# Raw memory rows into the first projections, their row norm behind them, and the first transfers reordered

## What is computed

```
def rms_norm_2(x, gain):
    y = xf * lax.rsqrt(jnp.mean(xf * xf, axis=-1, keepdims=True) + EPS)
    return y * gain
mem_kv = rms_norm_2(mem, mem_norm) @ mem_wkv            # 256 x 1024 @ 1024 x 2048
mem_k, mem_v = jnp.split(mem_kv, 2, axis=-1)
mem_k = rms_norm_2(mem_k.reshape(bsz, MEM_LEN, MEM_HEADS, MEM_HEAD_DIM), mem_knorm)
```

## Time and profile before

| what | value |
|---|---|
| median of 3 timed runs | 1941.95 us (1940.13 to 1942.1) |
| profiled execution, its own time | 1947.68 us |
| its span, first to last instruction | 1945.9 us |
| mean granted TensorE clock | 0.975 |
| TensorE busy | 1867.0 us, 96% of the span |
| VectorE busy | 1265.8 us, 65% |
| ScalarE busy | 898.9 us, 46% |
| GpSimd busy | 109.9 us, 6% |
| moved by the transfers | 311.34 MB, 160 GB/s in the mean |

### The profile page before, as it was taken

The page is one execution under the profiler, slowest core; times in us unless marked ns, Lnnn a source line. Parts: engine busy times, 40 slices in busy tenths (PEclk is TensorE's granted clock), DMA queues, the critical chain, the costliest instruction groups (busy, mean ns, idle before and its releaser), DMA issues.

```text
span 1945.9 us, 31345 instructions
## 1 busy us (share of the span) xinstructions
PE 1867.0 (96%) x12538; PEld 1681.6 (86%) x12551; DVE 1265.8 (65%) x1569; ACT 898.9 (46%) x1082; POOL 109.9 (6%) x79
## 2 busy tenths in 40 slices
PE   6988999998999998999999999999999998899999
PEld 6975899987589997999898888999999987789998
DVE  5786877788787677555667655555655567556555
ACT  5544544444454445333554455333433357545332
POOL 0300200030020000000034000000000000000000
PEclk9996999999699999999999999999999998999999
DMA  9540465554046554555442544555555542335553
GB/s 299 187 140 13 145 223 178 175 162 147 8 146 217 193 176 134 191 193 177 132 148 87 202 166 138 188 193 180 177 194 176 190 152 87 110 107 174 183 183 129
DMA packets 227044, 311.34 MB, mean 160 GB/s; under 512 B 6614, under 2 KB 199414, under 8 KB 226326
## 3 DMA queue, kind: packets, MB, share of 16 engines
q1 hardware_dynamic: 224038, 298.07, 45.9%
q0 software_dynamic: 2640, 10.66, 1.7%
q10 hardware_dynamic: 288, 1.54, 0.2%
HBM read 307.09 MB, written 3.15 MB: 159 GB/s over the span
## 4 chain that ended last, share of the span: by engine, by line
PE 88%; DVE 6%; ACT 4%; issue 2%; DMA 1%; DVEq 0%; ACTq 0%
PE bank L681 46%; PE bank L937 18%; PE bank L833 7%; PE bank L704 4%; PE bank L690 3%; PE bank L1003 1%; PE bank L979 1%; PE bank L737 1%; DVE w_lo L2038 1%; DVE work L2035 1%; ACT w_hi L1473 1%; DVE work L2038 1%; PE bank L990 1%; DVE x L2035 1%; PE bank L1127 1%
## 5 line engine op out<-in xcount | busy, mean ns | idle before, releaser
L2038 DVE TENSOR_TENSOR w_lo<-raw,w_hi 128x2048 fp32r<-128x2048 f32 x280 | 643.5, 2307 | 343.7 <-ACT w_hi L1473 343.2
L1473 ACT ACTIVATE w_hi<-raw 128x2048 fp32r<-128x2048 f32 x280 | 532.8, 1904 | 675.7 <-PE bank L681 431.9
L681 PE MATMUL bank<-xt_hi,w_hi 128*128 128x256 f32 x2544 | 723.4, 284 | 4.9 <-DVE w_lo L2038 3.3
L681 PE MATMUL bank<-xt_hi,w_lo 128*128 128x256 f32 x2544 | 721.2, 283 | 0.0
L681 PE MATMUL bank<-xt_lo,w_hi 128*128 128x256 f32 x2544 | 721.1, 283 | 0.0
L681 PEld LDWEIGHTS bank<-xt_hi,w_hi 128*128 128x128 f32 x2544 | 489.0, 192 | 9.3 <-issue 3.7
L681 PEld LDWEIGHTS bank<-xt_lo,w_hi 128*128 128x128 f32 x2544 | 489.0, 192 | 2.4 <-issue 0.2
L681 PEld LDWEIGHTS bank<-xt_hi,w_lo 128*128 128x128 f32 x2544 | 488.9, 192 | 0.0
L937 PE MATMUL bank<-w_hi,act_hi 128*128 128x512 f32 x528 | 206.5, 391 | 0.0
L937 PE MATMUL bank<-w_lo,act_hi 128*128 128x512 f32 x528 | 206.2, 390 | 0.0
L937 PE MATMUL bank<-w_hi,act_lo 128*128 128x512 f32 x528 | 205.5, 389 | 0.0
(11 more groups left out here) (307 smaller groups left out, 2108.6 us busy)
## 6 DMA issues: line engine op xcount, KB each, us to landing
raw<-in_ffn_wi SPq DMA_DIRECT2D x88, 1024.0 KB, 5.1
raw<-in_ffn_w_up SPq DMA_DIRECT2D x44, 1024.0 KB, 5.1
raw<-in_ffn_wo SPq DMA_DIRECT2D x44, 1024.0 KB, 4.9
raw<-in_ffn_w_down SPq DMA_DIRECT2D x22, 1024.0 KB, 5.4
raw<-in_w_in SPq DMA_DIRECT2D x14, 1024.0 KB, 5.4
raw<-in_ssd_in_proj SPq DMA_DIRECT2D x14, 1024.0 KB, 5.2
raw<-in_mem_wkv SPq DMA_DIRECT2D x9, 1024.0 KB, 8.1
raw<-in_w_out SPq DMA_DIRECT2D x8, 1024.0 KB, 5.1
```

What stands on the lines that cost most here:

```text
L681: ins = first(mm(dst, w[s][:, k, c0:c0 + m], xt[v][:, k, :], start=k == 0 and p == 0, stop=k == KT - 1 and p == 2))
L1473: return act.activation(dst, src, ACT.Copy)
L2038: return dve.tensor_tensor(out=out, in0=in0, in1=in1, op=op)
```

## The change

The memory rows are turned as they land, without their norm. The gain of each feature is applied as before, when the banks are emptied. The norm of a row is the same factor r for all of a row's products, so it can be applied later. For the values, tokens lie on partitions, and ScalarE multiplies by r (`rcol`) while it empties the bank, in two instructions instead of one. For the keys, r drops out of the norm of each head if epsilon is divided by r squared: TensorE adds epsilon times (mean square of the row + epsilon), held in `vcol`, to each mean of squares by two products of the broadcast column with the identity, and the root is taken without a bias. The sums of squares and their root move on ScalarE behind the splits of mem0 and mem1; VectorE's reciprocal moves behind its own.

SP issues mem0 right behind `memx`, ahead of the small parameters, and then waits until mem0 has landed before it issues mem1. ScalarE issues the constants behind the split of mem0. The early parameters are turned into bank 4 instead of bank 0.

```diff
--- before.py
+++ after.py
@@ -523,6 +523,7 @@
         row_ready = sem("row_ready")
         qsum_ready = sem("qsum_ready")
         even_rows = sem("even_rows")
+        mem_scale = sem("mem_scale")
         gain_ready = sem("gain_ready")
         zgate_ready = sem("zgate_ready")
 
@@ -861,8 +862,12 @@
                     ins.then_inc(bank_full[b], 1)
 
                 pe.wait_ge(early_in, 16 * EARLY_DMAS)
-                turn_parameters(0, 0, range(1))
-                turn(memx, "mem")
+                turn_parameters(4, 0, range(1))
+                for b in range(4):
+                    claim(b, f"mem.t{b}")
+                pe.wait_ge(memx_in, 16)
+                for tt, h in ORDER:
+                    turn_half(memx, tt, h)
                 turned("mem")
                 for j in range(4):
                     pair_fm(f"mem{j}", j % 2, f"memk{j}")
@@ -883,8 +888,13 @@
                 pe.wait_ge(sq_ready, seen.next(sq_ready))
                 b = 4 + h % 2
                 claim(b, f"{tag}.ms{h}")
+                pe.wait_ge(mem_scale, 1)
+                for tt in range(TT):
+                    mm(bank[b][:, P * tt:P * tt + P], vcol[:, tt:tt + 1].broadcast_to([P, P]), ident,
+                       start=True, stop=False, skip_group_check=True)
                 for c in range(2):
-                    ins = mm(bank[b][:, 0:T], cst("mean256"), sq[:, 2 * h + c, :], start=c == 0, stop=c == 1)
+                    ins = mm(bank[b][:, 0:T], cst("mean256"), sq[:, 2 * h + c, :], start=False, stop=c == 1,
+                             skip_group_check=True)
                 ins.then_inc(bank_full[b], 1)
 
             def norm(tag, l):
@@ -1521,13 +1531,6 @@
             def start():
                 act.dma_start(con[:, 0:P], consts[:, 0:P]).then_inc(ident_in, 16)
                 act.wait_ge(ready, 1)
-                act.wait_ge(memx_in, 16)
-                act.dma_start(con[:, P:], consts[:, P:cols["pick"][0]]).then_inc(const_in, 16)
-                for tt in range(TT):
-                    step(act.activation(z[:, tt, :], memx[:, tt, :], ACT.Square, accum_out=st[:, tt:tt + 1]))
-                    act.activation(st[:, 2 + tt:3 + tt], st[:, tt:tt + 1], ACT.Sqrt, scale=1.0 / D,
-                                   bias=eps[:, 1:2]).then_inc(sd_ready, 1)
-
                 def take_parameters(first, n):
                     b = full(f"par{first}")
                     drained(f"par{first}", copy(par[:, first:first + n, :], b[:, 0:P * n]))
@@ -1535,8 +1538,13 @@
 
                 take_parameters(0, 1)
                 split()
+                act.dma_start(con[:, P:], consts[:, P:cols["pick"][0]]).then_inc(const_in, 16)
                 take_stream("mem", lambda k: par_col("mem_norm_2", k))
                 split()
+                for tt in range(TT):
+                    step(act.activation(z[:, tt, :], memx[:, tt, :], ACT.Square, accum_out=st[:, tt:tt + 1]))
+                act.activation(st[:, 2:2 + TT], st[:, 0:TT], ACT.Sqrt, scale=1.0 / D,
+                               bias=eps[:, 1:2]).then_inc(sd_ready, 1)
                 for j in range(9):
                     if j < 8:
                         split()
@@ -1545,7 +1553,11 @@
                         drained(f"memk{j - 1}", copy(mem_k[:, 2 * j - 2:2 * j, :], b[:, :]))
                     elif j > 4:
                         b = full(f"memv{j - 5}")
-                        drained(f"memv{j - 5}", copy(mem_v[:, :, 256 * (j - 5):256 * (j - 5) + 256], b[:, :]))
+                        act.wait_ge(mem_scale, 1)
+                        for tt in range(TT):
+                            ins = act.activation(mem_v[:, tt, 256 * (j - 5):256 * (j - 5) + 256],
+                                                 b[:, 256 * tt:256 * tt + 256], ACT.Copy, scale=rcol[:, tt:tt + 1])
+                        drained(f"memv{j - 5}", ins)
                     if j == 3:
                         for tt in range(TT):
                             act.wait_ge(var_ready, seen.next(var_ready))
@@ -1567,7 +1579,7 @@
 
             def deviation(tag, h):
                 b = full(f"{tag}.ms{h}")
-                drained(f"{tag}.ms{h}", act.activation(x_sd[:, h, :], b[:, 0:T], ACT.Sqrt, bias=eps[:, 1:2]))
+                drained(f"{tag}.ms{h}", act.activation(x_sd[:, h, :], b[:, 0:T], ACT.Sqrt))
 
             def norm(tag, l):
                 if tag in ("mix", "ffn"):
@@ -2155,15 +2167,14 @@
                 dve.memset(eps[:, 2:3], 64 * RMS_EPS)
                 dve.memset(a_pad[:, :, :], 0.0)
                 dve.memset(zero[:, :], 0.0).then_inc(ready, 1)
-                for tt in range(TT):
-                    dve.wait_ge(sd_ready, seen.next(sd_ready))
-                    step(dve.reciprocal(rs[:, tt:tt + 1], st[:, 2 + tt:3 + tt]))
-                    dve.tensor_scalar(memx[:, tt, :], memx[:, tt, :], rs[:, tt:tt + 1], None,
-                                      ALU.mult).then_inc(z_ready, 1)
                 taken("par0")
                 split()
                 take_stream("mem", lambda k: par_col("mem_norm_2", k))
                 split()
+                dve.wait_ge(sd_ready, seen.next(sd_ready))
+                dve.reciprocal(rcol[:, :], st[:, 2:2 + TT])
+                dve.tensor_scalar(vcol[:, :], st[:, 0:TT], RMS_EPS / D, RMS_EPS * RMS_EPS, ALU.mult,
+                                  ALU.add).then_inc(mem_scale, 1)
                 for j in range(8):
                     split()
                     if j == 2:
@@ -2848,7 +2859,6 @@
             def start():
                 pool.wait_ge(x_in, 16 * TT)
                 load_wide(inp["ln_in_g"], inp["ln_in_b"])
-                seen.next(z_ready, TT)
 
                 pool.wait_ge(mem_ready, 4)
                 pool.dma_start(mem_dram[0], work[:, WORK - 4096:WORK - 2048]).then_inc(mem_out, 16)
@@ -2986,12 +2996,15 @@
 
             def start():
                 sp.dma_start(memx[:, :, :], inp["mem_2"][0].rearrange("(t p) d -> p t d", p=P)).then_inc(memx_in, 16)
+                columns("mem0", inp["mem_wkv_2"], 0, 256)
                 sp.wait_ge(stage_clear, 1)
                 for dst, src in stage_loads(True):
                     sp.dma_start(dst, src).then_inc(early_in, 16)
+                sp.wait_ge(landed[0], 16)
                 late, sent = stage_loads(False), 0
                 for j in range(8):
-                    columns(f"mem{j}", inp["mem_wkv_2"], 256 * j, 256)
+                    if j >= 1:
+                        columns(f"mem{j}", inp["mem_wkv_2"], 256 * j, 256)
                     if j == 2:
                         for tt in range(TT):
                             sp.dma_start(x[:, tt, :], inp["x"][0, P * tt:P * tt + P, :]).then_inc(x_in, 16)
```

## The result

The changed kernel's median is 1944.25 us (22 runs, 1939.89 to 1950.17) against 1941.09 for the kernel before, measured beside it (22 runs, 1936.13 to 1946.07). The ratio is 1.0023, with a 95% interval of 1.0014 to 1.0032: slower. The medians are 3.2 us apart and the means, of which the ratio is made, 4.5; 2.7 was forecast. Its profiled execution took 1943.42 us with a span of 1941.6, and that span is 4.3 us shorter than the one before.

What follows compares the result with a forecast made beforehand. TensorE, with 88% of the chain, was taken as the bound, so only its stops and added instructions count. +1.0 us at memk3 and +1.7 for products gave +2.7 on 1941.95: 1944.7 us, range 1941.0 to 1946.8.

Steps and rivals of the forecast that it cites:

- the products (+1.7): At the four mean squares, two added products each, 0.43 us a pair, lengthen TensorE's path by 1.7 us.
- the stop at memk3 (+1.0): Ahead of memk3 TensorE waits 1.5 us for memk1's copy, so memk3 begins 1.0 us later than before.
- More than 0.2% slower: Case that the whole kernel gets slower by over 0.2%, which is 3.9 us; chance 0.15.
- Part 1: Start of TensorE: parameters land with mem0, taken as 10.4 us; TensorE starts 0.5 us earlier, at 18.3.
- Part 2: ScalarE's squares, table load and root behind mem1's split, 3.9 us together, are hidden with 1.6 us to spare.
- Part 3: SP's wait for mem0 idles the transfers 3.5 us; mem4 lands 2.45 later, at 36.1, and memk3 begins 1.0 later.
- The hole in the transfers: While SP waits for mem0 before issuing mem1, the engines have nothing from 8.4 to 11.9 us, 3.5 us.
- mem4 is not late: Rival at memk3: wide rows let mem4 go first or the hole is shorter; +1.2 us, 1943.2; chance 0.2.
- Part 4: Products added at the four mean squares put 4 x 0.43 = 1.7 us on TensorE's path; bounds 1.7 and 2.4.

Runs made afterwards that it cites:

- e6: Changed kernel with the first transfers in the order of the kernel before (parameters, mem0, mem1 without wait), norm still deferred: median 1941.64 us, ratio 1.0007.
- e8: e6 with one pair of epsilon products, added by VectorE, and memk0 to memk3 emptied ahead of the next split: median 1942.87 us, ratio 1.0003.
- e11: e8 with the late parameters turned into banks 6 and 7: median 1942.20 us, ratio 0.9999.
- e12: e11 with bf16 products of zeros in TensorE's two stops, twelve in the first and nine in the second: median 1938.10 us, ratio 0.9981.
- e3: Changed kernel without the eight epsilon products in the norm of the memory keys: median 1942.74 us, ratio 1.0006.
- e5: Changed kernel without SP's wait for mem0, mem0 still ahead of the parameters: median 1944.51 us, ratio 1.0018.
- e7: Changed kernel with nine bf16 products of zeros on TensorE between the turn of the memory rows and mem0: median 1943.72 us, ratio 1.0015.
- e10: Changed kernel with nine bf16 products of zeros behind the turn of the memory rows and nine behind the turn of x: median 1943.17 us, ratio 1.0005.
- e2: Kernel before with only the eight products of a broadcast column added ahead of the four mean squares: median 1943.92 us, ratio 1.0015.
- e4: Changed kernel run again, unchanged: median 1944.14 us, ratio 1.0013.
- e1: Kernel before run again, unchanged, as a control: median 1941.79 us, ratio 0.9995.

## Why the prediction held, and where not

**Direction and size.** Forecast +2.7 us and 1944.7; measured 1944.25, ratio +0.23%. That the numbers meet is luck in part: of the sum's two terms the products (+1.7) were about right, the stop at memk3 (+1.0) didn't happen, and slow products that the sum didn't have filled its place. More than 0.2% slower had been given 0.15, and the ratio lies there, if barely. The sum began from a spread of 2 us, read from three runs, where 22 runs spread by 10; and the range of 1941.0 to 1946.8 adds 0.2 and 0.4 at its ends, not the 2 that the text says.

**Part 1, the start: right in its mechanism, 0.9 us off in a landing.** The parameters land with mem0 behind which they were put: 9.52 us instead of 6.82, and e6, e8, e11 and e12 show that this alone takes 1.4 to 2.3 us from the start. I said 10.4, since I took mem0's landing from the kernel before; with nothing queued behind it, it landed at 9.0. The start came at 17.63 to 17.77, not 18.3. The edit meant to bring the first unit forward holds it back.

**Part 2, the work moved behind: right.** w_lo of mem2 is done at 28.97, TensorE asks at 30.72. The last mem_v evictions were costed at nothing beside the fourth pair and cost 0.10 us (0.25 in e3, without the pair).

**Part 3, mem4 late: this step failed.** I had memk3 begin 1.0 us later than before; it began 1.07 earlier (36.48 against 37.55) with no stop. mem4 landed at 33.2, not at 36.1. The hole in the transfers was 2.1 us and not 3.5, because mem0 landed sooner and SP acted at 8.99; the idle third in 23 to 26 us took up half of it; and the wide rows, 85% of the engines in 26 to 28 us before, now went behind SP's units. That was the rival "mem4 is not late", at +1.2 us, with both of its reasons. e5 shows the wait to be worth nothing for a TensorE as late as this one. The banks behind mem3 and mem4 are real limits, as e7 and e10 show (two stops, 1.0 and 0.85 us together), but only for a TensorE that comes earlier than 36 us to memk3.

**Part 4, the products: right, 1.4 us for 1.7.** The fourth pair is mostly hidden (e2). That they make the whole kernel slower is shown by e2 alone; without them (e3) the kernel isn't to be told from the one before.

**What was missing: the clock of mem0.** I took mem0's 7.24 us as given. It is not: the kernel before has 5.99, 7.24 and (with the products, e2) 8.68; the changed one has 7.33 to 7.87, where TensorE stands still for 4.1 us instead of 2.1 behind its transpositions. That fillers there give 5.8 to 6.0 every time is shown, in four profiles. That the changed kernel draws the lower clock more often than the kernel before is not: the 1.6 us of the split rest on its first 22 runs, with no clocks of before beside them, and the fillers of e10 brought no gain that the timed runs show. Where in the span the rest of that clock is lost, apart from mem0 and the 7.47 us behind the turn of x in e4 and e5, is open.

## What to carry to other kernels

A small transfer that everything waits for belongs ahead of a large one on the same queue; moved behind a unit of 1 MB, four rows cost 1.4 to 2.3 us of start, against the 2.0 to 3.5 that the deferred norm had won (18.30 or 18.79 against 15.31 to 16.26). Work taken off the path in front of TensorE can leave it standing longer in one piece, and its next products may then run at the lower clock; a few products of zeros in the gap cost nothing there and kept the full clock, though only e12 has a timed gain to go with it. And before a shorter start is counted as a gain, look for the next bank or landing with little slack, here 1.45 us at memk3.

## What the runs showed of the hardware

- The same program takes 41.5 or 38.0 us for one attention stage (kernel before, first profile and e1), with a granted clock of 0.50 or 0.67 from 160 to 170 us; the changed kernel has 36.6 at 0.84. Timed runs of one kernel spread by 10 us and fall by 1.16 us for each 0.001 of mean granted clock, and one profile of each kernel can show the opposite sign of the measured difference.
- The clock column can read 1.00 beside slow products (ten start in 2 us of the kernel before, nineteen in e1). The distance between the starts of products, 0.21 or 0.12 us, is the surer sign.
- mem0 landed by 8.96 to 9.26 us (five profiles, by SP's next issue) with only the parameter rows queued behind it. With mem1 behind it, it landed at 9.39, 10.00, 10.29 and 10.34 in e6, e8, e11 and e12 and at 10.45 in the kernel before. A landing read from one profile is good to about 1 us here.
- The queue of SP let x's two transfers through in 2.10 us here (10.05 on), while they took 6.17 us of SP's time in the kernel before.
